# Up projection of a hybrid layer: one 512-column matmul for both activation halves, the halves added by VectorE, the conv taps read from SBUF

## The reference, cut to what matters

```python
D_MODEL = 2048; SEQ = 256; GRID_W = 64; D_FF = 5632

def dwconv2d_grid(x, w):
    B, T, C = x.shape
    rows = T // GRID_W
    y = lax.conv_general_dilated(x.reshape(B, rows, GRID_W, C), w[:, :, None, :],
                                 window_strides=(1, 1), padding=((1, 1), (1, 1)),
                                 dimension_numbers=('NHWC', 'HWIO', 'NHWC'),
                                 feature_group_count=C)
    return y.reshape(B, T, C)

def conv_glu_ffn(h, w_up, conv_w, w_down, grid):
    up = h @ w_up                                   # (256, 2048) @ (2048, 11264)
    up = dwconv2d_grid(up, conv_w)
    a, b = jnp.split(up, 2, axis=-1)
    return (jax.nn.silu(a) * b) @ w_down            # (256, 5632) @ (5632, 2048)
```

## Time and profile before

| | us |
|---|---|
| median of 3 runs | 2997.85 (2994.82 to 2999.31) |
| the profiled execution | 2995.07 |
| its span | 2993.1 |
| mean granted TensorE clock | 0.979 of full speed |
| busy over the span: PE / PEld | 2841.4 (95%) / 2207.5 (74%) |
| busy: DVE / ACT / POOL | 1839.5 (61%) / 1002.5 (33%) / 579.6 (19%) |
| one pass of the up phase (four tiles) | 23.04, 22 passes |

### The profile page before, as it was taken

How to read it: one execution, slowest core, us unless ns; L and a number is a source line. 1 busy time by engine, 2 the same in 40 slices (tenths; PEclk the granted TensorE clock), 3 DMA queues, 4 the chain that set the end, 5 groups by cost and what they waited for, 6 DMA issues and landing times.

```text
span 2993.1 us, 70020 instructions
## 1 busy us (share of the span) xinstructions
PE 2841.4 (95%) x27808; PEld 2207.5 (74%) x27808; DVE 1839.5 (61%) x3324; ACT 1002.5 (33%) x1715; POOL 579.6 (19%) x708
## 2 busy tenths in 40 slices
PE   5899999999999999999989999999989999999997
PEld 1246665566656566666556699999979999999997
DVE  1115666677666767666675544444378888885434
ACT  1123322333322333332231433333354444443333
POOL 0003222333122233222231110000013333330000
PEclk9799999999999999999999999999989999999998
DMA  8621332222332222233214545554525555554553
GB/s 323 268 77 63 107 107 93 70 74 89 103 107 93 82 75 86 93 106 107 79 53 148 204 148 182 186 182 170 198 99 183 182 182 182 182 182 156 182 174 134
DMA packets 75291, 412.28 MB, mean 138 GB/s; under 512 B 9200, under 2 KB 11888, under 8 KB 42736
## 3 DMA queue, kind: packets, MB, share of 16 engines
q1 hardware_dynamic: 74352, 407.51, 39.5%
q0 software_dynamic: 768, 2.10, 0.2%
HBM read 405.38 MB, written 4.19 MB: 137 GB/s over the span
## 4 chain that ended last, share of the span: by engine, by line
PE 84%; DVE 8%; issue 3%; DMA 3%; ACT 1%; SPq 0%; DVEq 0%; ACTq 0%; PEldq 0%
PE PB L671 18%; PE Q L919 6%; PE Q L920 6%; PE Q L924 6%; PE PB L919 4%; PE PB L920 4%; PE PB L924 4%; PE CH L924 3%; PE CH L920 3%; PE CH L919 3%; DMA ring<-w_mod_dram 3%; PE Q L808 3%; PE PB L656 2%; PE Q L794 2%; PE Q L815 2%
## 5 line engine op out<-in xcount | busy, mean ns | idle before, releaser
L671 PE MATMUL PB<-hT,ring 128*128 128x512 f32 (+1 forms) x1536 | 673.5, 552 | 6.4 <-PEq L660 5.4
L1615 DVE TENSOR_TENSOR w_lo_r<-ring,w_hi_r 128x1536 fp32r<-128x1536 f32 (+3 forms) x178 | 386.9, 2174 | 269.8 <-ACT w_hi_r L1217 269.8
L1217 ACT ACTIVATE w_hi_r<-ring 128x2048 fp32r<-128x2048 f32 (+2 forms) x178 | 325.8, 1831 | 453.7 <-PE Q L924 211.3
L671 PEld LDWEIGHTS PB<-hT,ring 128*128 128x128 f32 x1536 | 256.8, 189 | 120.9 <-issue 70.7
L920 PE MATMUL PB<-hT_r,w_hi_r 128*128 128x256 f32 x832 | 204.6, 285 | 0.0
L1475 DVE SCALAR_TENSOR_TENSOR arena<-ring,csilp,arena 128x512 f32<-128x512 f32 x240 | 193.5, 806 | 5.2 <-DMA ring<-w_mod_dram 1.0
L1775 DVE TENSOR_TENSOR w_lo_r<-ring,w_hi_r 128x1408 fp32r<-128x1408 f32 x62 | 101.2, 1633 | 147.9 <-ACT w_hi_r L1331 147.9
L1876 POOL TENSOR_TENSOR w_lo_r<-ring,w_hi_r 128x512 fp32r<-128x512 f32 x88 | 118.4, 1346 | 361.4 <-ACT w_hi_r L1217 361.4
L919 PE MATMUL PB<-hT_r,w_hi_r 128*128 128x256 f32 x704 | 175.7, 289 | 4.7 <-DVE hT_r L1702 4.7
L919 PE MATMUL Q<-ff_hi_r,w_hi_r 128*128 128x256 f32 x704 | 175.6, 288 | 1.8 <-ACT w_hi_r L1331 1.8
L920 PE MATMUL Q<-ff_lo_r,w_hi_r 128*128 128x256 f32 x704 | 172.9, 284 | 0.0
(11 more groups left out here) (266 smaller groups left out, 6096.5 us busy)
## 6 DMA issues: line engine op xcount, KB each, us to landing
ring<-w_up_dram SPq DMA_DIRECT2D x88, 1024.0 KB, 4.8
ring<-w_mod_dram SPq DMA_DIRECT2D x128, 512.0 KB, 3.7
ring<-w_rkv_dram SPq DMA_DIRECT2D x48, 1024.0 KB, 5.8
ring<-w_down_dram SPq DMA_DIRECT2D x64, 704.0 KB, 4.0
ring<-w_mod_dram SPq DMA_DIRECT2D x32, 1024.0 KB, 7.8
ring<-w_ga_dram SPq DMA_DIRECT2D x16, 1024.0 KB, 4.8
ring<-w_gb_dram SPq DMA_DIRECT2D x16, 1024.0 KB, 4.8
ring<-w_pa_dram SPq DMA_DIRECT2D x16, 1024.0 KB, 4.8
```

The costliest lines, as they stand in the source:

```text
L671: last = mm(PB[slot % 2][:, 0:cols], tile(n, kt), hT[:, kt, 0:cols], start=(kt == 0), stop=(kt == KT - 1))
L1217: f(w_hi_r[:, r % 2, 0:n], ring[:, r, 0:n], ACT.Copy).then_inc(hi_rdy, 1)
L1615: tt(w_lo_r[:, r, 0:n], ring[:, r, 0:n], as_f32(w_hi_r[:, r % 2, 0:n]), ALU.subtract).then_inc(lo_rdy, 1)
```

## The change

The low activations and the high ones are streamed by one matmul of 512 columns per slice kt with the high weight, `hT_r[:, kt]` whole, into the whole bank: columns 0 to 255 get weight high times activation low, columns 256 to 511 weight high times activation high. The 16 matmuls with the low weight add to columns 256 to 511. The two halves of the bank must then be added. ACT copies columns 0 to 255 to an SBUF buffer `us[r]` (tensor woven, free since the RWKV phase), and DVE adds columns 256 to 511 to it. The centre tap (ACT) and the eight side taps (DVE) read `us[r]` and not the bank. TensorE may write a bank again when its add is done (`up_sum`), and no longer when the taps are. ACT has to wait for the taps before it writes `us[r]` again.

```diff
+        us = [woven_sb[:, r].rearrange("p c t -> p (c t)")[:, 0:T] for r in range(4)]
+        up_half = sem("up_low_activation_half_copied")
+        up_sum = sem("up_halves_added")
 ...
@@ TensorE @@
+            pe.sem_inc(up_sum, 4)
             def up_four(i, first):
                 for r in range(4):
                     high_ready("up", i, r)
-                    pe.wait_ge(up_cv, i * 2 + 1 + r // 2)
+                    pe.wait_ge(up_sum, i * 4 + r + 1)
                     for kt in range(KT):
                         if first and r == 0:
                             pe.wait_ge(h_rdy, KT + kt + 1)
-                        with_high(four[r][:, 0:T], r, kt, h2_hi_r[:, kt], h2_lo_r[:, kt], kt == 0)
+                        mm(four[r][:, :], w_hi_r[:, r % 2, kt * P:(kt + 1) * P], hT_r[:, kt], start=(kt == 0), stop=False)
                     low_ready("up", i, r)
                     pe.wait_ge(up_lo, i * 4 + r + 1)
                     for kt in range(KT):
-                        last = with_low(four[r][:, 0:T], r, kt, h2_hi_r[:, kt], kt == KT - 1)
+                        last = with_low(four[r][:, T:TT], r, kt, h2_hi_r[:, kt], kt == KT - 1)
@@ ScalarE @@
                     if r % 2 == 0:
+                        act.wait_ge(up_cv, i * 2 + r // 2 + 1)
                         act.wait_ge(ff_rdy, i * 2 + r // 2 + 1)
-                    f(cv[r], four[r][:, 0:T], ACT.Identity, scale=convw_a[:, r, 4:5]).then_inc(up_mid, 1)
+                    f(us[r], four[r][:, 0:T], ACT.Copy).then_inc(up_half, 1)
+                    act.wait_ge(up_sum, i * 4 + r + 5)
+                    f(cv[r], us[r], ACT.Identity, scale=convw_a[:, r, 4:5]).then_inc(up_mid, 1)
@@ VectorE @@
             def taps(i, j, half, prev):
-                if half == 0:
-                    dve.wait_ge(up_mid, i * 4 + 2 * j + 2)
 ...
-                        if n:
+                        if n == 0:
+                            dve.wait_ge(up_mid, i * 4 + r + 1)
+                        else:
                             V.need(prev[q])
-                        last = stt(grid(cv[r])[:, orow, ocol], grid(four[r][:, 0:T])[:, irow, icol],
+                        last = stt(grid(cv[r])[:, orow, ocol], grid(us[r])[:, irow, icol],
                                    convw_v[:, r, w:w + 1], grid(cv[r])[:, orow, ocol], ALU.mult, ALU.add)
+            def add_halves(i, r):
+                dve.wait_ge(up_half, i * 4 + r + 1)
+                tt(us[r], us[r], four[r][:, T:TT], ALU.add).then_inc(up_sum, 1)
 ...
                     taps(i - 1, 1, 1, carry)
+                add_halves(i, 0)
                 lows("up", i, 0, FT // 2, "down")
 ...
+                add_halves(i, 1)
                 prev = taps(i, 0, 0, [0, 0])
                 lows("up", i, 1, FT // 2, "down")
                 if carry is not None:
                     gated(i - 1, 1)
                 taps(i, 0, 1, prev)
+                add_halves(i, 2)
                 lows("up", i, 2, FT // 2, "down")
+                add_halves(i, 3)
                 prev = taps(i, 1, 0, [0, 0])
```

## The result

The changed kernel takes 3063.18 us, the median of 4 runs (3060.94 to 3063.85); the kernel before takes 2998.44 (4 runs, 2994.82 to 2999.31). The ratio is 1.0217, with a 95% interval of 1.0199 to 1.0235. The forecast was 3065, range 3010 to 3095. The profiled execution has a span of 3061.8 us, 68.7 more than before: the up phase, from its first matmul to its last, went from 515.6 us (2195.4 to 2711.0) to 575.6 (2199.6 to 2775.2), which is +60.0; what follows it went from 282.1 to 286.6, +4.5; the remaining 4.2 lies in phases that the change doesn't touch.

What follows compares the result with a forecast made beforehand. TensorE bounds the kernel at 23.04 us a pass, VectorE nearly full behind it. VectorE would then set 26.3: 20 passes give +65, the end +5, so +70 on 2995.07 makes 3065, range 3010 to 3095.

Steps and rivals of the forecast that it cites:

- The taps collide with GpSimd: VectorE's up-phase taps, now with two SBUF inputs, are blocked by each GpSimd instruction that reads SBUF, for its own length.
- up to 6.36 of blocking: GpSimd's 7.48 us in an up-phase pass, less 8 leads of 0.14, all costing VectorE; 2.08 already paid in the subtractions.
- The 26.3 of the forecast: Up-phase pass in us, set by VectorE: a sum of 26.7 less 0.4, against TensorE's 21.5.
- -0.4: Taken off VectorE's 26.7 us pass: adds and waits are 7% of it, and GpSimd costs nothing in them.
- The two rules: Skill rules on VectorE's taps: two SBUF inputs contend with GpSimd; overhead is 58 cycles from SBUF, 120 from PSUM.
- The rival built on it (3022): Up-phase taps some 0.065 us cheaper from SBUF, pass 24.2 us, time 3022; chance 0.14, shared with half the further blocking.
- half of the further blocking: Same rival's other case: only half of GpSimd's added blocking of VectorE, pass 24.2 us, time 3022; chance 0.14, shared.
- Under a long stream the load is hidden: TensorE's up-phase 512-column matmul hides its weight load: 0.216 us each, pass 21.5, worth up to 34 us alone.
- the first rival: Up-phase taps don't collide with GpSimd: blocking stays 2.08, pass 21.9 us bound by VectorE, time 2973; chance 0.10.
- VectorE without the collision: VectorE's up-phase pass with no further blocking: 18.51 + 2.08 + 1.3 = 21.9 us.
- The ends: Up phase's first pass -1.5 us, second +1.5; last SiLU and TensorE's stop before the down phase +5.
- Clock: Rival: TensorE's clock falls to half in a fifth of the up-phase passes, +60 us, time 3125; chance 0.06.

Runs made afterwards that it cites:

- e1: Changed kernel with the taps' other operand, cv, in PSUM and the down phase's output in other banks; 2979.01 us, ratio 0.9939 to the kernel before.
- e2: Changed kernel with the add writing its sum back into the bank, where centre tap and side taps read it; 2980.15 us, ratio 0.9944 to the kernel before.
- e3: Kernel before, with ScalarE copying each bank to SBUF and the side taps reading the copy; 3016.05 us, ratio 1.006 to the kernel before.
- e4: Changed kernel without GpSimd's low-weight subtractions in the up phase, ScalarE copying those columns unsubtracted; 2979.16 us, ratio 0.9943 to the kernel before.
- e7: Changed kernel with GpSimd's share of the low-weight subtraction given to VectorE, 2048 columns in place of 1536; 3013.13 us, ratio 1.0061 to the kernel before.
- e6: e1 with high-weight matmuls streaming 384 columns and low-weight ones loading 64 weight columns, but for each tile's last; part of the product left out; 2966.34 us.

## Why the prediction was right

The forecast came out within 2 us of the median, and its mechanism is the one that e1, e2, e3, e4 and e7 show. That it came so close is partly luck, as the ends below tell. By its own steps:

- **The taps collide with GpSimd.** Shown. VectorE's pass was put together as 18.51 without any blocking, plus adds, waits and up to 6.36 of blocking. Measured: the subtractions gave back 2.09 a pass (4 x (2.275 - 1.753)) where 2.08 was reckoned; the taps took 5.5 more; four adds of 0.41 stand 0.33 apart, 1.3; two waits of 0.26, 0.5. So 20.59 - 2.09 + 5.5 + 1.3 + 0.5 = 25.8, and the trace has 26.07; 0.3 is not accounted for. The 26.3 of the forecast was 0.2 too long. Its -0.4 was too small and had the wrong reason: in the pass above no GpSimd instruction lies beside an add or a wait, so these spared VectorE nothing. Each GpSimd subtraction costs 1.05 where 1.16 was reckoned. The CAST and the instruction behind it cost 0.65 together (eight taps from 2473.40 to 2477.81 take 4.41 in place of 2.72, less 1.04 for the subtraction) where 0.87 was reckoned. 4 x 1.05 + 2 x 0.65 is the 5.5. Part of the difference is that GpSimd bears some of the loss itself: its CAST went from 0.40 to 0.70 and the instruction behind it from 0.75 to 0.88.
- **The two rules.** The taps' record grew from 0.40 to 1.44 and 1.52 beside GpSimd, and one operand in PSUM took the means of up to 0.973 back to 0.47. The Trainium skill, SBUF — State Buffer, section "Who interferes with whom", has two SBUF inputs on VectorE contend with a GpSimd instruction that reads SBUF. By that rule, the traces agree. A 189-column tap that meets no GpSimd takes 0.40 from either memory. The Trainium skill, VectorE: DVE Perf Modes, section "The TRN2 errata", has an SBUF input cheaper than a PSUM one; the traces don't show it. The rival built on it (3022) falls. Its other reading, half of the further blocking, falls too: 5.5 of 6.36 were paid.
- **TensorE.** This step was wrong, and it did not matter. "Under a long stream the load is hidden" gave 0.216 for a 512-column matmul. It is 0.227: (2408.81 - 2405.16) / 16 = 0.228 in e1. The 13.3 ns that a 256-column matmul takes beyond its columns stay at 384 and 512 columns, so TensorE's own pass is 22.27 and not 21.5, and the change can win 0.77 us a pass, 17 us in all, not 34. The evidence was from float32 matmuls at two cycles a column, another type. Had the first rival come true, the pass would have been 22.27 by TensorE and not 21.9 by VectorE; e1's 2979 beside the rival's 2973 shows that (its terms give 2972: 1.14 x 22 is 25, not 24).
- **VectorE without the collision.** The rival's 21.9 has its match in e6's 21.92, but not by its terms. VectorE is busy for 21.36 us of that pass and waits for the rest, which the rival left out, and the subtractions pay 4 x (2.125 - 1.76) = 1.5 for GpSimd and not 2.08.
- **The ends.** At the start of the phase the forecast had one pass shorter by 1.5 and one longer by 1.5. From one first matmul of a pass to the next, the first pass is shorter by 0.6 (31.28 for 31.84) and the second longer by 0.2 (23.25 for 23.04). The first gains less since the 512-column matmul saves less, and VectorE's lateness reaches TensorE by the second. The 20 others have some 26.07, +60.6 in place of +65. After the phase it is +4.5 against +5: up to the end of the long stop TensorE is 3.9 later, 2.1 of it in that stop and most of the rest in two new stops of 0.51 and 0.57 ahead of it, and 0.6 come from a slightly longer stretch at half clock. The +60.0 of the phase and the 4.5 make 64.5, so the forecast of +70 was 5.5 too much. The profiled difference is 68.7 all the same, as 4.2 lie in phases that the change doesn't touch; the medians differ by 64.7. What brought the forecast to the median is its starting point: the profiled execution's 2995.07 lay 3.4 under the median of 2998.44. That is luck.
- **Clock.** 1.00 in every 100 us from 2300 to 2700, as forecast. Half clock stands only over the first matmuls of the phase, as before the change, and behind the stop at its end.

The best kernels here are e1 and e2 (2979 and 2980, 17 to 18 us under the kernel before): the one 512-column matmul is a gain of 0.77 us a pass, if the taps keep an operand in PSUM.

## What to carry to other kernels

Before moving an operand from PSUM to SBUF, count the SBUF inputs of the VectorE instruction that reads it and see what GpSimd does at that time: here each 1.3 us of subtraction on GpSimd then cost VectorE 1.05, though neither's price alone had changed. An engine that is 90% busy and not the bound decides what a gain elsewhere is worth; work out its period with the change before counting the gain. Where a helper engine gets in the way of the one that it helps, compare the time that it takes from it (1.1 us here) with the work that it takes off it (0.53); here doing without it won 50 us.

## What the runs showed of the hardware beyond that

- At full clock a matmul of this type with its own weight load steps by its columns at 2.4 GHz plus a constant: 0.120, 0.173 and 0.227 us at 256, 384 and 512 columns, with 13.3 ns beyond the columns each time at 128 weight columns, and 0.1135 at 256 columns with 64 weight columns, 6.8 ns beyond. As far as two widths can tell, that is some 0.104 ns per weight column (an estimate, 13.3 / 128) that a longer stream doesn't hide. At half clock it doesn't show: 13 steps of 256 columns behind the stop, 2789.40 to 2792.17, take 0.213 each, which is 256 columns at 1.2 GHz. Nor does it with float32, where 0.002 is left. What makes it is open.
- A busy share of VectorE is no measure of its work: in e4 and e1 it is 96 of 100 with 194 instructions, in the changed kernel 97.5 with 166. The count beside the busy time shows the blocking.
